# One masked score tile for each head instead of a stack of level tiles, filled by predicated copies

## The reference

```python
diff = G[:, :, None] - G[:, None, :]          # G: cumulative log decay
decay = jnp.exp(jnp.where(causal, diff, -jnp.inf))
scores = jnp.einsum('bthk,btshk->btsh', qb, decay * kb[:, None])
o_intra = jnp.einsum('btsh,bshv->bthv', scores, vb)
```

## Time and profile before

| | us |
|---|---|
| median of 3 runs | 1763.25 |
| lowest and highest | 1761.62, 1763.91 |
| the profiled execution's own time | 1763.15 |
| its span, first to last instruction | 1761.2 |
| TensorE busy | 1699.5 |
| VectorE busy | 1282.2 |
| ScalarE busy | 1039.1 |

### The profile page before, as it was taken

How to read it: one execution, slowest core, us unless ns; L and a number is a source line. 1 busy time by engine, 2 the same in 40 slices (tenths; PEclk the granted TensorE clock), 3 DMA queues, 4 the chain that set the end, 5 groups by cost and what they waited for, 6 DMA issues and landing times.

```text
span 1761.2 us, 23315 instructions
## 1 busy us (share of the span) xinstructions
PE 1699.5 (96%) x9594; PEld 1479.7 (84%) x9594; DVE 1282.2 (73%) x1207; ACT 1039.1 (59%) x942; POOL 98.5 (6%) x85
## 2 busy tenths in 40 slices
PE   8999889999999999889999999999999999999997
PEld 7988778999999978678888888888888888788876
DVE  6635755444347356659988898988888888888897
ACT  4444333333234344257777777777777777777776
POOL 2001120000000011204100000000000000000200
PEclk9998989999999989899999999999999999999999
DMA  9549163443544422259999999999999999899994
GB/s 299 167 148 286 49 191 120 144 139 113 155 156 135 155 45 68 60 184 363 401 395 396 396 375 386 369 385 394 356 384 375 369 396 393 311 392 373 374 394 174
DMA packets 272616, 474.07 MB, mean 269 GB/s; under 512 B 41578, under 2 KB 103266, under 8 KB 272504
## 3 DMA queue, kind: packets, MB, share of 16 engines
q1 hardware_dynamic: 266432, 452.37, 72.3%
q10 hardware_dynamic: 3368, 12.75, 2.2%
q0 software_dynamic: 2704, 7.39, 1.5%
HBM read 454.69 MB, written 29.84 MB: 275 GB/s over the span
## 4 chain that ended last, share of the span: by engine, by line
PE 90%; DVE 6%; issue 2%; ACT 2%; DMA 1%; ACTq 0%; DVEq 0%
PE ps L1718 16%; PE ps L1719 16%; PE ps L2361 11%; PE ps L1713 9%; PE ps L1714 9%; PE ps L2382 5%; PE ps L1812 4%; PE ps L2247 3%; PE ps L1929 2%; DVE spL L1598 1%; PE ps L2265 1%; PE ps L1907 1%; PE ps L2400 1%; PE ps L2209 1%; DMA ring<-in_w_exp_in_dram 1%
## 5 line engine op out<-in xcount | busy, mean ns | idle before, releaser
L1598 DVE TENSOR_TENSOR spL<-ring,spH 128x2048 fp32r<-128x2048 f32 x336 | 767.3, 2293 | 100.4 <-ACT spH L966 97.5
L966 ACT ACTIVATE spH<-ring 128x2048 fp32r<-128x2048 f32 x336 | 643.0, 1916 | 132.2 <-PE ps L2361 69.5
L1718 PE MATMUL ps<-spH,XH 128*128 128x512 f32 x896 | 354.4, 395 | 1.8 <-issue 1.8
L1719 PE MATMUL ps<-spH,XL 128*128 128x512 f32 x896 | 350.4, 391 | 0.0
L1049 DVE TENSOR_TENSOR spL<-ring,spH 128x2048 fp32r<-128x2048 f32 (+1 forms) x74 | 158.8, 2146 | 182.3 <-ACT spH L661 182.1
L1713 PE MATMUL ps<-hnH,spH 128*128 128x320 f32 x928 | 277.2, 313 | 4.0 <-DVE hnL L1064 2.2
L1714 PE MATMUL ps<-hnL,spH 128*128 128x320 f32 x928 | 275.5, 311 | 0.0
L661 ACT ACTIVATE spH<-ring 128x2048 fp32r<-128x2048 f32 (+1 forms) x74 | 133.4, 1803 | 187.8 <-PE ps L2247 73.6
L2361 PE MATMUL ps<-spL,XH 128*128 128x512 f32 x896 | 241.2, 391 | 1.4 <-DVE spL L1598 1.1
L2361 PEld LDWEIGHTS ps<-spL,XH 128*128 128x128 f32 x896 | 168.0, 188 | 38.8 <-DVE spL L1598 2.4
L1718 PEld LDWEIGHTS ps<-spH,XH 128*128 128x128 f32 x896 | 168.7, 188 | 36.0 <-issue 2.2
(11 more groups left out here) (364 smaller groups left out, 1772.5 us busy)
## 6 DMA issues: line engine op xcount, KB each, us to landing
ring<-in_w_exp_in_dram SPq DMA_DIRECT2D x224, 1024.0 KB, 8.5
ring<-in_w_exp_out_dram SPq DMA_DIRECT2D x112, 1024.0 KB, 8.8
ring<-in_w_in_dram SPq DMA_DIRECT2D x28, 1024.0 KB, 5.3
ring<-in_w_ffn_in_dram SPq DMA_DIRECT2D x22, 1024.0 KB, 5.1
token_rows<-token_rows ACTq DMA_DIRECT2D x1, 11776.0 KB, 41.2
ring<-in_w_ffn_out_dram SPq DMA_DIRECT2D x16, 704.0 KB, 4.6
ring<-in_w_out_dram SPq DMA_DIRECT2D x8, 1024.0 KB, 5.0
out_dram<-ring SPq DMA_DIRECT2D x32, 256.0 KB, 2.9
```

The source lines that it names most:

```text
L966: A(esplit(j)[0], src, ACT.Copy).then_inc(S("hi_done"), 1)
L1598: V.tensor_tensor(lo, eslot(j)[0], hi.bitcast(F32), ALU.subtract).then_inc(S("split_done"), 1)
L1718: mm(out, x[0], w, start=start, stop=False)
L1719: return mm(out, x[1], w, start=False, stop=False)
```

## The change

The plain tile, whose mask holds the diagonal and levels 5 and 6 (for a sample head the diagonal alone), is multiplied by its mask first, into a single tile of 128 x 128 (64 x 64). Then for each lower level v a predicated copy writes the level's scores from PSUM over that tile. It covers only the columns t that lie in the right half of their block, which is half of the columns (`later`), and writes where the mask is not zero. Every one of these instructions waits for the one before by `own`; the last signals `sc_done`. The output product is then one matmul for a head in place of six or four. The mask tables hold only the columns that are read. The tile SC takes n columns, and its old room is kept, so that the tiles behind it stay where they were relative to it.

```diff
--- before.py
+++ after.py
@@ -87,7 +87,9 @@
     parts = {
         "w": wp.reshape(P, -1), "l": lp, "ws": ws.reshape(NS, -1), "ls": lspad,
         "id": np.eye(P), "ones": np.ones((P, P)),
-        "mask": np.concatenate([mp[:, :LOW], mp[:, LOW:].sum(1, keepdims=True)], 1).reshape(P, -1), "ms": ms.reshape(NS, -1), "seq": seq, "turn": turn,
+        "mask": np.concatenate([mp[:, LOW:].sum(1)] + [mp[:, v, (i >> v) % 2 == 1] for v in range(LOW)], 1),
+        "ms": np.concatenate([ms[:, LS]] + [ms[:, v, (i[:NS] >> v) % 2 == 1] for v in range(LS)], 1),
+        "seq": seq, "turn": turn,
         "iota": np.tile(i[None, :], (P, 1)), "before": (i[:, None] < i[None, :]),
     }
     at, n = {}, 0
@@ -98,6 +100,11 @@
     for k, v in parts.items():
         out[:v.shape[0], at[k][0]:at[k][0] + v.shape[1]] = v
     return out, at
+
+
+def later(x, v):
+
+    return x.rearrange("p (g r b) -> p g r b", r=2, b=1 << v)[:, :, 1]
 
 
 def unit_plan():
@@ -246,7 +253,8 @@
         Y = put("Y", [P, LV, P])
         cursor[0] += 4 * 1024 + 512
         sc0 = cursor[0]
-        SC = put("SC", [P, LV + 1, P])
+        SC = put("SC", [P, P])
+        cursor[0] += 3584
         qG = put("qG", [P, H, NS])
         egl = put("egl", [P, H, NSQ])
         egp = put("egp", [P, H])
@@ -266,7 +274,7 @@
         hn0 = base + 4 * KT * TOK
         Mb = [M, put("M1", [P, LV + 1, P], offset=hn0)]
         Yb = [Y, put("Y1", [P, LV, P], offset=hn0 + 4 * 1024)]
-        SCb = [SC, put("SC1", [P, LV + 1, P], offset=hn0 + 11 * 1024 + 512)]
+        SCb = [SC, put("SC1", [P, P], offset=hn0 + 11 * 1024 + 512)]
         ea = put("ea", [P, NSQ * NH], offset=hn0 + 15 * 1024 + 512)
         am = put("am", [P, NSQ, NH], offset=hn0 + 15 * 1024 + 768)
         kd2 = put("kd2", [NS, H * P], offset=hn0 + 16 * 1024)
@@ -1261,13 +1269,18 @@
                     dve.wait_ge(S("sc_mm"), j + 1)
                     if j >= 2:
                         dve.wait_ge(S("o_mm"), j - 1)
-                    SCv = flat(SCb[h % 2])[:, 0:((LOW if t < 2 else nl) + 1) * n]
-                    if t < 2:
-                        V.tensor_tensor(SCv, ps[:, 2:4, :].rearrange("p b n -> p (b n)")[:, 0:(LOW + 1) * n], tabv("mask"),
-                                        ALU.mult).then_inc(S("sc_done"), 1)
-                    else:
-                        V.tensor_tensor(SCv[0:n], ps[0:n, 2, 0:(nl + 1) * n], tabv("ms")[0:n], ALU.mult
-                                        ).then_inc(S("sc_done"), 1)
+                    low = LOW if t < 2 else LS
+                    sc = SCb[h % 2][0:n, 0:n]
+                    raw_sc = ps[0:n, 2:4, :].rearrange("p b n -> p (b n)")
+                    mask = tabv("mask" if t < 2 else "ms")[0:n]
+                    own(V.tensor_tensor(sc, raw_sc[:, low * n:(low + 1) * n], mask[:, 0:n], ALU.mult))
+                    for v in range(low):
+                        mine = mask[:, n + v * n // 2:n + (v + 1) * n // 2].bitcast(I32)
+                        ins = V.copy_predicated(later(sc, v), mine.rearrange("p (g b) -> p g b", b=1 << v),
+                                                later(raw_sc[:, v * n:(v + 1) * n], v))
+                        if v < low - 1:
+                            own(ins)
+                    ins.then_inc(S("sc_done"), 1)
 
                 def step_gates(t):
                     n = TILES[t][1]
@@ -1924,10 +1937,7 @@
                     if h == 0 and t != ORDER[0]:
                         pe.wait_ge(S("o_evac"), i)
                     out = ps[:, 6, h * n:(h + 1) * n]
-                    top = LOW if t < 2 else nl
-                    for v in range(top + 1):
-                        m = mm(out, vtk_of(t)[0:n, h * P:(h + 1) * P], flat(SCb[h % 2])[0:n, v * n:(v + 1) * n],
-                               start=v == 0, stop=v == top and t != 1)
+                    m = mm(out, vtk_of(t)[0:n, h * P:(h + 1) * P], SCb[h % 2][0:n, 0:n], start=True, stop=t != 1)
                     if t == 1:
                         if h == 0:
                             pe.wait_ge(S("sh_done"), 2 * l + 1)
```

## The result

The changed kernel takes 1772.5 us (median of 5 runs, 1770.5 to 1777.2) against 1763.1 for the kernel before (median of 5), a ratio of 1.005 with the interval [1.003, 1.007]. It is slower by about 9 us, where 1762.4 and no change to be told were forecast, and it lies above the range's end of 1769. Of all the runs in this document one, of the kernel before on the chip of e_six_matmuls, took 3600 us and is left out.

The account below looks back on a forecast made before the run. TensorE was taken to set the pace, with VectorE's longer masked step cancelling most of its saving: 1763.15 - 2.8 (gains at entries and last heads) + 2.1 (clock falls) = 1762.4 us, range 1757 to 1769.

Parts of the forecast that it names:

- Layer 0's entry: Layer 0's sample tile before the first prompt head: the last output product, at half clock, gets 1.45 us shorter.
- rival 4: Prompt heads: the masked step isn't the next bound and TensorE's saving stays; faster, chance 0.22 together with Rival 1.
- The ring of the second prompt tile: Each head's closed chain through scores, masked step, state addition and state product: 5.92 us forecast against 5.94 before.
- R: Length of VectorE's masked step for a prompt head: one product plus five waited copies, 1.54 us, bounds 1.21 to 1.91.
- One fall a layer: First prompt tile, after head 2's idle 3 us: TensorE drops to half clock, 1.05 us lost a layer, 2.1 together.
- Rival 3: Slow clock in each layer's loop lasts beyond one 3.4 us stretch: 1765.8, with two more 1769; chance 0.13.
- the prediction's slope: All sixteen prompt masked steps are on the new path, so each 0.1 us of R is worth 1.6 us.
- Rival 2: All sixteen prompt steps: a predicated copy takes two passes over its columns, 0.37 us more each, 1768.4; chance 0.20.
- shifted whole: Experts' phase: starts earlier or later by the loop's shift, with no change of its own booked.
- The gain of 0.5 us behind the last head of each layer: After the second prompt tile's last head: shorter output product brings state matmuls about 0.7 us earlier, 0.5 gained a layer.
- layer 1's entry: Layer 1's sample tile before the first prompt head: the shorter last output product gains about 0.3 us.
- Rival 1: Copies cheap or waits free: 1757.1, at unwaited cadence 1753.6, without the clock's fall 1751.5; chance 0.22 together with rival 4.

Follow-up runs that it names:

- e_six_matmuls: Changed kernel with tiles at the old addresses, output product again six (sample head four) matmuls, all over the one tile; 1778.7 us, ratio 1.0079 to the kernel before.
- c_one_matmul: Kernel before with its one masked product of all tiles, but the output product takes the plain tile alone, lower levels left out; 1747.4 us, ratio 0.9916.
- g_two_copies: Changed kernel, old addresses, prompt heads with a four-tile product, two predicated copies (levels 0 and 1) and four matmuls; 1759.25 us, ratio 0.9972 to the kernel before.
- d_filled: Changed kernel at old addresses, plus unneeded matmuls where TensorE waits for the masked step at four prompt heads; 1761.4 us, ratio 0.9996 to the kernel before.
- a_room_kept: Changed kernel with 416 unused columns behind the table, so later tiles keep their old addresses; 1767.0 us, ratio 1.0032 to the kernel before.
- b_own_tiles: Changed kernel at old addresses, each copy writing its own unread tile, without waits between product and copies; 1750.0 us, ratio 0.9928 to the kernel before.

## Why the prediction was wrong

**What held.** VectorE becomes the bound from the first masked step of the first prompt tile on; no wait stands between its instructions there. TensorE waits 3.0 us before the output product of head 2, the number forecast. Layer 0's entry gained 1.4 us (1.45 forecast). Every prompt masked step is on the path, which answers rival 4. The ring of the second prompt tile is scores, masked step, state addition or output product, state product, and its price in each kernel is the same sum with another step: 2.01 + R + 1.18 + 1.09 + 0.1 gives 6.12 for R = 1.74 (6.16 measured) and 5.34 for R = 0.96 (c_one_matmul, 5.38). With four matmuls or six the output product, longer than the state addition, takes the third term: g_two_copies 5.90, e_six_matmuls 6.74.

**The sum, term by term** (us, profiled executions):

| | forecast | measured |
|---|---|---|
| before the first prompt head of layer 0 | -1.45 | -1.4 |
| between the masked steps of both layers, clock at 1.00 | 0 | +2.4 |
| falls of the clock there | +2.1 | +6.3 |
| from layer 0's last prompt head to layer 1's first | -0.8 | -3.4 |
| from layer 1's last prompt head to the experts | -0.5 | +0.3 |
| the experts' stage | 0 | +3.1 |
| sum | -0.7 | +7.3 |

The three terms that failed are the clock, the step R and the experts' stage.

**The clock (largest).** One fall a layer was booked, at 1.05 us each. There were two in each: the second near 191 and 690 us, at the end of the second prompt tile, behind a wait of 1.8 us before the output product and 0.5 before the state product. The prediction had walked the first tile head by head and summed the second as a ring, so it didn't see what idle time of TensorE the ring leaves. By the distances of d_filled the first fall cost 1.9 us in layer 0 and 0.9 in layer 1, the second 1.35 and 2.2: 6.3 us together, against 2.1. Rival 3 was about length, and was right in part: two of the four slow stretches lasted 6.8 to 6.9 us instead of 3.4, and these are the two dearest.

**The size of R.** The term that was mis-sized is the copy, 214 ns taken from a row of contiguous columns: it measured 255 in the mean, 0.30 for the two levels with the finest strides and about 0.23 for the other three. R is 1.74 instead of 1.54, within its bounds of 1.21 to 1.91. By the prediction's slope that is 16 x 0.20 = 3.2 us; with the clock up (d_filled) the heads of both layers took 2.4 us more than before. Rival 2 named the right place and point of decision (a copy with its gap over 0.30 us), but the copies came to 0.29 with it, and no second pass is needed to explain them.

**The experts' stage.** The prediction booked nothing for the smaller table but its transfer, and said that the experts' phase is "shifted whole". The smaller table moves all tiles behind it by 1664 bytes, and the stretch of 28 activations runs 0.75% slower for it, 3.6 us, of which 0.5 came back behind it. Without the move (a_room_kept, 1767.0) the change is inside the range but slower by 0.3%, not the same.

**What offset the errors.** The gain of 0.5 us behind the last head of each layer wasn't there: in layer 1 the state matmuls (L1943, now L1953) start 3.07 us behind the last masked step, where they started 2.90 behind it, since the longer step and the state addition now stand on the path in place of the output product. On the other side layer 1's entry gained 1.6 us, where 0.3 was booked (the first prompt head's scores hold the chain for 1.12 us instead of 1.95), and 1.8 us came back behind layer 0's loop, where a slow stretch of the clock is gone. Neither was foreseen; that they took 2.6 us off the loss is luck.

**Rival 1.** The outcome that the prediction drew from the Trainium skill's rule on semaphores (copies at the unwaited cadence) didn't come. b_own_tiles shows that this cadence exists (0.94 us for the six), but only where nothing waits for anything. The rule itself says no more than that both forms take the same time, and for these copies they don't.

## What to carry to other kernels

Replacing matmuls by short dependent VectorE instructions can buy TensorE's time at more than its price when the loop is a ring through both engines: sum the ring, with every hand-over, for the kernel before and after, and look for the mix at which the longest two paths meet (here, of those that were run, two copies and four matmuls, not five and one). Time that an engine is relieved of appears as idle time, and on TensorE idle time can cost the clock as well, so list its waits for each stretch of the new order. And a change of a table's size is a change of every later tile's address: keep the room before comparing anything else, and try a few places for buffers that feed TensorE.

## What the runs showed of the hardware

- The place of weight buffers in SBUF changes the pace of the experts' matmuls: 384 bytes up for three of the buffers made 28 turns of the experts' loop take 481.6 us instead of 477.6, at a granted clock of 1.00 in both.
- A predicated copy of 64 columns from PSUM takes 0.23 us when it writes runs of four columns or more, and 0.30 us when it writes single columns or pairs. Five of them take 0.74 us without waits and into separate tiles, and 1.42 us with waits into one tile.
- TensorE's clock fell behind waits of 3.0 us, behind waits of 1.8 and 0.5 us close together, and in e_six_matmuls behind one of 1.8 us; behind waits of 1.2 and 1.5 us in g_two_copies it stayed at 1.00, but c_one_matmul, with the same wait of 1.5 us at head 2 in both layers, lost it in layer 1 (0.71 at 648 to 652 us) and not in layer 0. Matmuls without use in those waits kept it at 1.00 and left the other distances between heads as they were.
